# One decoder step on one core: the first norm worked tile by tile in the opening stage, the second at the end of the layer before it, and in the attention stage the sigmoids issued head by head and the value quarters spread over a turn

## The reference, cut to what matters

```
h = x
# layer 0: gated matrix-memory mixer
h = h + mlstm(rmsnorm(h, norm_mix[0]) @ w_in_a, state) @ w_out_a
h = h + square(relu(rmsnorm(h, norm_mlp[0]) @ w_up[0])) @ w_down[0]
k, v = rmsnorm(h, norm_kv) @ w_kv               # shared, 16 heads of 64
# layer 1: stick-breaking attention over cached pages and new keys
q = rmsnorm(h, norm_mix[1]) @ w_q_b
z = q @ k.T / 8 + bias
A[t, s] = sigmoid(z[t, s]) * prod_{s<j<t} (1 - sigmoid(z[t, j]))
h = h + (A @ v) @ w_out_b
h = h + square(relu(rmsnorm(h, norm_mlp[1]) @ w_up[1])) @ w_down[1]
y = rmsnorm(h, norm_final)
```

## Time and profile before

| what | before |
|---|---|
| median of 3 runs | 3087.38 us (3086.38 to 3090.63) |
| the profiled execution's own time | 3094.23 us |
| its span, first to last instruction | 3092.4 us |
| PE busy | 2893.2 us, 94% of the span |
| mean granted PE clock | 0.974 |

### The profile page before, as it was taken

The page is one execution under the profiler, slowest core; times in us unless marked ns, Lnnn a source line. Parts: engine busy times, 40 slices in busy tenths (PEclk is TensorE's granted clock), DMA queues, the critical chain, the costliest instruction groups (busy, mean ns, idle before and its releaser), DMA issues. The chain is left out here.

```text
span 3092.4 us, 49344 instructions
## 1 busy us (share of the span) xinstructions
PE 2893.2 (94%) x19749; PEld 2634.2 (85%) x19749; DVE 1378.7 (45%) x1993; ACT 818.4 (26%) x1647; POOL 756.2 (24%) x452
## 2 busy tenths in 40 slices
PE   5999997999999999978999899898799999999998
PEld 4989887999999999976766677666599999999997
DVE  4422334444433344444546554655545433344434
ACT  3120222211110011124555545555512110011112
POOL 4212111322323323332111211120122332332331
PEclk8999998999999999989999999999899999999999
DMA  5666444233233232223333433343411111111112
GB/s 160 177 149 193 83 29 92 73 92 96 81 95 95 81 95 87 89 97 96 107 109 98 121 97 114 100 119 91 147 48 42 48 42 47 47 41 47 47 41 77
DMA packets 362482, 277.68 MB, mean 90 GB/s; under 512 B 31394, under 2 KB 353954, under 8 KB 360290
## 3 DMA queue, kind: packets, MB, share of 16 engines
q1 hardware_dynamic: 341002, 258.18, 28.8%
q10 hardware_dynamic: 21336, 17.47, 2.9%
HBM read 251.58 MB, written 91.11 MB: 111 GB/s over the span
## 5 line engine op out<-in xcount | busy, mean ns | idle before, releaser
L162 POOL CAST w_hi<-w_raw 128x1024 fp32r<-128x1024 f32 x194 | 208.6, 1075 | 1661.1 <-PE bank L214 902.0
L212 PE MATMUL bank<-p_u_hi,w_hi 128*128 128x352 f32 x1536 | 496.5, 323 | 14.5 <-DVE p_u_lo L2001 14.5
L212 PE MATMUL bank<-x_hi,w_hi 128*128 128x352 f32 x1536 | 496.9, 323 | 2.9 <-DVE p_q L1758 2.9
L213 PE MATMUL bank<-p_u_lo,w_hi 128*128 128x352 f32 x1536 | 495.5, 323 | 0.0
L214 PE MATMUL bank<-p_u_hi,w_lo 128*128 128x352 f32 x1536 | 495.3, 322 | 0.0
L214 PE MATMUL bank<-x_hi,w_lo 128*128 128x352 f32 x1536 | 494.5, 322 | 0.0
L213 PE MATMUL bank<-x_lo,w_hi 128*128 128x352 f32 x1536 | 494.0, 322 | 0.0
L164 POOL TENSOR_TENSOR w_lo<-w_raw,w_hi 128x1024 fp32r<-128x1024 f32 x194 | 483.8, 2494 | 15.6
L2009 DVE TENSOR_TENSOR h<-bank,h 128x352 f32<-128x352 f32 x384 | 199.9, 524 | 492.5 <-PE bank L214 492.5
L1961 ACT ACTIVATE p_relu<-bank 128x352 f32<-128x352 f32 x192 | 89.1, 464 | 1039.5 <-PE bank L214 1033.2
L212 PEld LDWEIGHTS bank<-p_u_hi,w_hi 128*128 128x128 f32 x1536 | 288.5, 188 | 18.7 <-issue 18.7
(11 more groups left out here) (247 smaller groups left out, 4587.7 us busy)
## 6 DMA issues: line engine op xcount, KB each, us to landing
k_pages<-in_cache_k SPq DMA_DIRECT2D x64, 512.0 KB, 5.7
w_raw<-in_w_up SPq DMA_DIRECT2D x64, 512.0 KB, 4.0
v_pages<-in_cache_v SPq DMA_DIRECT2D x64, 512.0 KB, 4.8
w_raw<-in_w_down SPq DMA_DIRECT2D x64, 512.0 KB, 3.4
p_pages<-k_pages SPq DMA_DIRECT2D x256, 128.0 KB, 2.4
p_pages<-v_pages SPq DMA_DIRECT2D x256, 128.0 KB, 2.3
w_raw<-in_w_in_a SPq DMA_DIRECT2D x26, 512.0 KB, 4.5
h<-h_spill ACTq DMA_DIRECT2D x16, 528.0 KB, 8.6
```

Of the source, the lines that this page charges most:

```text
L162: pool.tensor_copy(m.whi[slot][:, :], m.wraw[slot][:, :]).then_inc(w.hi, 1)
L212: pe.matmul(bank[:, 0:TW], wh, xh, start=(k == 0), stop=False)
L213: pe.matmul(bank[:, 0:TW], wh, xl, start=False, stop=False)
```

## The change

Four parts.

**Start.** `constants` and `embed` become one stage, `start`. The rows of `x` are the first transfers, the first weight panel comes in after the third block of them, one gain goes out on ACT's queue, the rest at the end of SP's. ACT copies two of every three turned halves, DVE one. As soon as the tokens of a tile of 352 are there, ACT and DVE make its `x_hi` and `x_lo` and PE its share of the gate product (banks 5 to 7); squares are added per tile. Ln and Exp of the norm stand at the stage's end, and SP writes the copy of `h` that the next stage needs. `mixer_a` no longer has a norm or the unused second panel, and takes its first dense tile (TAU0) ahead of the gate rows.

**Handover.** In layer 0's MLP the last of the 8 turns is written out. In it ACT and DVE follow each finished block `k` with `x_hi`, `x_lo`, square and sum, SP stores the block, and PE ends the stage with `dense_first` for `mixer_b` in banks 5 to 7, the sum over partitions (banks 2 to 4) ahead of its last two blocks. `mixer_b` begins with tile 3.

**Sigmoids.** ACT's sigmoids for a chunk are issued one head at a time with a turn's copy in between, where both heads' stood together.

**Order in a slot.** In slots 1 and 5 the value quarters stand after turns 0, 1 and 3 and at the end, where they stood after turns 0 to 3. In slots 0 and 4 DVE takes `chain_of` of the first chunk ahead of `chain_sample`.

```diff
+    VALUES_AFTER = {0: [0], 1: [1], 3: [2]}
...
-                    if i < len(quarters):
-                        values(*quarters[i])
+                    for x in VALUES_AFTER.get(i, ()):
+                        if x < len(quarters):
+                            values(*quarters[x])
...
-                if tiles:
-                    gates(p, n, 0)
+                due = [(x, h2) for x in range(len(CHUNKS[n])) for h2 in range(2)] if tiles else []
+                if due:
+                    gates(p, n, *due.pop(0))
                 for i, y in enumerate(turns):
                     read_turn(y)
-                    if i == 1 and lower:
-                        gates(p, n, 1)
+                    if due and (due[0][0] == 0 or i):
+                        gates(p, n, *due.pop(0))
...
-                for pc, g in at(SUMS_AT, slot):
-                    chain_sample(pc, g)
                 done = []
...
                 if p < PAIRS:
                     chain_of(p, n, 0)
+                for pc, g in at(SUMS_AT, slot):
+                    chain_sample(pc, g)
...
+            if norm_after:
+                turn(CH - 1, 0)
+
+                def sums():
+                    pe.wait_ge(w.tile_free[2], USES_OUT + CH * USES_C)
+                    norm_pe(pe, m, after.s, 2)
+                dense_first(pe, m, after.w, 0, 0, 0, after.s.x, between=sums, at=KT - 2, bank0=5)
...
+                    if ending:
+                        dve.wait_ge(after.s.hi, k + 1)
+                        dve.tensor_tensor(m.xlo[:, k, :], m.h[:, k, :], f32(m.xhi[:, k, :]), ALU.subtract).then_inc(after.s.x, 1)
+                        norm_add(dve, m, after.s, k)
...
+            for g in range(2 * TO[1]):
+                turn(g)
+            gates(0)
+            for g in range(2 * TO[1], 2 * NB):
+                turn(g)
+            gates(1)
+            pe.wait_ge(made, 2)
+            wait_taken(pe, 2 * NB)
+            sums(0)
+            gates(2)
+            sums(1)
+            sums(2)
...
+            copies(0)
+            high(0)
+            copies(1)
+            high(1)
+            square(0)
+            copies(2)
+            high(2)
+            square(1)
+            square(2)
+            act.wait_ge(made, 2)
+            norm_act_rs(act, m, s, 2)
```

More of the change, by code:

```diff
@@ L111, in weight_turns @@
         per, per_tiles = len(panels), sum(x[1] for x in panels)
-        assert per % 2 == 0
+        assert per % 2 == 0 or (turns == 1 and panels is stages[-1][1])
         def turn(i, last, n0=n, t0=tiles, panels=panels, per=per, per_tiles=per_tiles):
@@ L236, in dense_first @@
     for k in range(KT):
-        if k == KT // 2 and between is not None:
+        if k == at and between is not None:
             between()
@@ L363, in _ @@
                 keep(v, ALU.is_equal, NEG, j, [[SG, 2], [-1, SB], [0, ST]], 0)
[L365 to L371, removed]
-                    sp.dma_start(tile[:, :], src.rearrange("(k p) -> p k", p=P)).then_inc(landed, 16)
-            sp.dma_start(m.ptab[:, :], m.d["page_table"].rearrange("b (o g) -> o (b g)", o=1)).then_inc(landed, 16)
-            sp.wait_ge(landed, 16 * len(gains) + 16)
@@ L378, in embed @@
[L378 to L396 removed]
+            split(1)
@@ new lines, in sums @@
+            def sums(t):
+                pe.wait_ge(s.acc, t + 1)
+                pe.matmul(m.bank[2 + t][:, 0:TW], m.ones[:, :], m.acc[:, t * TW:(t + 1) * TW], start=True, stop=True)\
+                    .then_inc(s.sum, 1)
+            for g in range(2 * TO[1]):
[7 more added lines that the diff above has]
+            sums(0)
@@ L1603, in turns @@
                     z(p, n, 1)
-                for y in quarters[len(turns_of(slot)):]:
+                placed = sum(len(x) for i, x in VALUES_AFTER.items() if i < len(turns_of(slot)))
+                for y in quarters[placed:]:
                     values(*y)
@@ L1832, in _, with out_and_mlp @@
                         sample_queries(pq)
-def out_and_mlp(nc, m, own, w_out, w_up, w_down, gain, gather, head, after):
+def out_and_mlp(nc, m, own, w_out, w_up, w_down, gain, gather, head, after, norm_after):
     with ExitStack() as c:
@@ L1963, in _ @@
                         act.activation(sqr[t][:, :], relu[t][:, :], ACT.Square).then_inc(sq_ready, 1)
+            with act.Fori(0, CH - norm_after) as i:
+                turn(i)
+            if norm_after:
+                turn(CH - 1)
+                for k in range(KT):
+                    for t in range(NT):
+                        act.wait_ge(w.tile_free[t], USES_OUT + (CH - 1) * USES_C + UT + k + 1)
+                    act.activation(m.xhi[:, k, :], m.h[:, k, :], ACT.Copy).then_inc(after.s.hi, 1)
+                    norm_square(act, m, after.s, m.h, k)
+                norm_act_rs(act, m, after.s, 2)
         @block.vector
@@ L1991, in _, with turn @@
             dve.wait_ge(s.rs, 1)
-            with dve.Fori(0, CH) as i:
+            def turn(i, ending):
                 for u in range(UT):
```

312 lines of the change are left out of this document (192 added, 120 removed).

## The result

The changed kernel is slower: 3114.43 us median of 4 runs (3110.65 to 3117.24), where the kernel before took 3088.77 beside it. The ratio is 1.0083 (1.0065 to 1.0100), 25.7 us. The profiled execution took 3111.77 us with a span of 3110.0 us, 17.6 us more than before. Stage lengths are compared between the two profiled executions.)

What follows compares the result with a forecast made beforehand. PE was taken as the bound, busy 2893.2 us, so only its idle or low-clock stretches could shrink. -17 - 24.5 + 27 = -14.5 us from the median 3087.4 gave 3073 us, range 3030 to 3091 (8 in 10).

Steps and rivals of the forecast that it cites:

- quarters: Slots 1 and 5 of `mixer_b`: new places save 14 of 17.1 us of value-page waits; order in front costs 2 back.
- heads: Slot 3 of `mixer_b`: sigmoids by head shorten the `follow` wait and low clock, saving 17 us; slot 2 nothing.
- the discount: `mixer_b`: 13 us taken off the +40 loss, as other engines run on while PE waits at `sat`.
- Term 1: The start: earlier `x` transfers and norm work end the pick product near 52 us, -17 us, bounds -11 and -24.
- Term 2: Handover from layer 0's MLP to `mixer_b`: PE works on without the idle stretch, -24.5 us, bounds -20 and -27.
- 3 us of cover: Start of `mixer_b`: panel 2 is ready near 1374 us, before PE asks for it at 1377, so no wait.
- Term 3: `mixer_b`: savings in waits against a late `sat`, a net loss of +27 us, bounds -17 and +45.
- The wait at `sat`: Slots 0 and 4 of `mixer_b`: PE waits 6.6 and 2.9 us, 48 + 23 us; low clock adds 16.
- `chain_of` first: Slot 1 of `mixer_b`: weights and sigmoids found ready, saving 10 of 14.7 and 8 of 11.1 us of waits.
- Rival (b): `mixer_b` loses from 41.5 us on, as the `sat` wait is paid in full; 3096 us at +50; chance 0.11.
- full price of +40: `mixer_b`: sum of all its savings and losses, +40 us, before 13 us were taken off.
- Rival (a): `mixer_b`: without turn-taking `sat` is hardly late, a wait of 1.6, 35 us less loss, 3037 us; chance 0.27.

Runs made afterwards that it cites:

- e1: The changed kernel with DVE taking the sample's scan and product ahead of the heads' again in slots 0 and 4: 3044.92 us.
- e4: The changed kernel with DVE's order, quarter places and sigmoids by head all undone, leaving the new start and handover: 3061.98 us.
- e8: e1 with the three bias transfers moved behind the weight panels and the first eight page loads of `mixer_b`: 3041.32 us.
- e5: The changed kernel with the sample's work ahead of the heads' in slot 0 only: 3079.43 us.
- e3: The changed kernel with both heads' sigmoids issued together again: 3110.29 us.
- e11: e1 with the value quarters back behind turns 0 to 3, so sigmoids by head remain: 3055.76 us.
- e12: e1 with both heads' sigmoids together again, so the quarters' new places remain: 3047.03 us.
- e13: The changed kernel with POOL holding back slot 0's panel split until DVE's sample product is done: 3097.54 us.
- e6: The changed kernel with the sample's work ahead of the heads' in slot 4 only: 3078.10 us.

## Why the prediction was wrong, point by point

**In short.** The forecast was a gain of 14.5 us, the result a loss of 25.7. Three steps failed. By the medians of e1 and e4: start and handover gave 24.5 us where I had 41.5; DVE's order cost 69.5 where I had 48 + 23 - 18 + 16 = 69 and took 13 off, 56; quarters and heads together gave 17.1 (e4 against e1) where I had 14 - 2 + 17 = 29. (-24.5 + 69.5 - 17.1 = 27.9, against 25.7 in the first measurement.) The direction was lost by the discount together with the other two; with 69 in place of 56 alone the sum would still have been a gain, of 1.5 us.

**Term 1, right.** -17 predicted, -15.9 measured, with errors that cancel: the stage ended at 46.1 where I had 42, the picks began 6.4 us behind it where I had 7 to 9 and ended near 55 where I had 52, 14.2 us sooner than before; another 1.7 us came behind them.

**Term 2, its price.** Tile 3 came 36.1 us sooner, within the 35 to 45 that I gave, so 20.2 us without the start, where the working had 22.0. (22.0 and the 2.9 of clock are 24.9, not 24.5.) What failed is the next step, "what is late next is panel 2", with 3 us of cover. It sends the load out at 1361.3 + 1.9 and has landing and three passes done near 1374, 10.8 us later; POOL's passes took 5.5 after the change, so 5.3 were left for landing. The trace of before had this panel's landing at 13.3 us, and the same slow queue ahead of it:

```profile
1356.17 7.01 SPq L1372 DMA_DIRECT2D w_raw<-in_w_q_b  x1
...
w_raw<-in_w_kv SPq DMA_DIRECT2D x1, 512.0 KB, 13.3
```

With that row the cover of 3 us becomes a lack of 5. Before, the small bias transfers and the first panels were hidden behind PE's 37 us of waiting and `dense_first`; with these gone, the queue is what PE waits for: 5.56 us, and low clock behind it (0.87 up to the first scores, where e8 has 1.00). e8 shows the cause, since with the bias behind the pages the wait is gone and the first scores come 33.4 us behind tile 3 instead of 40.6 (34.7 before). The handover was worth 20.2 - 6.0 = 14.2 us up to the first scores, not 24.5; with the bias late it would be 20.2 + 1.3 = 21.5.

**Term 3, the discount.** The wait at `sat` was predicted in full: 48 + 23 = 71 us, measured 71.8 in 16. It was mostly 5.5 to 6.0 us in slot 0 and 2.8 in slot 4 where I had 6.6 and 2.9; the first pair had 7.6, and the last 4.5 and 5.0 where I had 2 and 2.9. The other rows: the waits for value pages gave 5.2 us for my 12; the heads 2.3 at `follow` and 6.4 at the cached pages, 8.7 for my 17; `chain_of` first 10.9 + 5.7 = 16.6 for my 18. The sum of the waits is 71.8 - 5.2 - 8.7 - 16.6 = 41.3 us, against 39.7 more idle time; with 9.1 of lower clock (I had 16) it makes the 48.9.

The step that failed is "part of what the late `sat` costs is slack elsewhere ... I take 13 off": nothing came off. e1 tests it, since it differs from the changed kernel in the order alone. The waits behind copies, from which I took the 13, are 36.0 us in e1 (21.3 + 5.3 + 9.4) and 36.9 with the late `sat` (22.0 + 5.5 + 9.4). What a late `sat` does take over is the waits at `pack` and the scores (22.0 us, e1), which my sum already had as the 18; and e5 shows that slot 4's wait takes over nothing. Without the discount the price of the order, 69, is what e1 measured, 69.5 us.

**Term 3, the heads.** This is the term that was mis-sized. What it named came: slot 3 went from 14.7 to 12.6 us in six pairs, 13.9 in all, though not by this edit alone (by head against together it is 8.0 with the new quarters). (The term's pieces, 1.1 of wait and 1.5 of clock, would be 2.6 and not 2.1.) Slot 2 was put at nothing, and nearly so it was: what the copies of cached pages gained there came back at `follow`. What has no term is that the same edit lengthens the waits for value pages and for the sigmoids by 9 us together. By the runs the heads lie between a loss of 4 us (e3) and a gain of 6 (e11 against e4), not 17. The quarters were priced rightly, 14 us of page waits (19.4 to 5.3, e4 and e12) and 10.6 to 15 by the runs for my 12; that only 5.2 of page waits went from before to after is the heads' doing.

**The rivals.** Rival (b) happened: from tile 3 to the output projection, as the prediction measures it, `mixer_b` is 897.9 us instead of 843.0, 54.9 more, of which 6.0 are the page wait and its clock. I gave it 0.11 although my own full price of +40 stood 1.5 us from its threshold. The argument against it, that a late PE lets the other engines catch up, had no row behind it. Rival (a)'s number for a world without turn-taking, a wait of 1.6 us in slot 0, is close to what e13 measured (1.40); but its 35 us do not follow, since the hold-up moves to the next scans. e1 shows what the whole change without this order is worth: 3044.9 us, and e8 3041.3, the fastest of the kernels run here.

## What to carry to other kernels

An instruction moved to the back of a queue costs its consumer the length of what now stands ahead, less the slack that it had, and that length is read at the place where it runs: beside a GpSimd pass VectorE's scans and products took two to three times as long. Slack that a new wait may use up is counted once, from the waits just behind it, and a wait that PE had not had before is priced with the lower clock behind it (71.6 us of stage time for 50.3 us of idle time). A copy that is made earlier is priced at the place where PE waits next, too. Where a barrier's cover is removed, the first transfers behind it are what can be late next, and their landing times are read from the trace that has them (13.3 us here), not taken as short because nothing waited for them.

## What the runs showed of the hardware

- Three transfers of the bias, 12 KB in all, ahead of two panels of 512 KB made the first panel land in 13.1 us instead of 5.5, and the second panel's issue took 6.10 us instead of 0.57 (the changed kernel and e8). Before had it too: 13.3 and 7.01 us.
- Waits of 1.65 and 1.85 us at the same place were followed by a granted clock of 1.00 and of 0.53 (e1 and e8). Of 10.2 us that e8 lost behind its first scores, 6.2 were busy time at the lower clock.
- The price of a wait followed the idle time that was left after what it took over: 24.3 us of waits in slot 4 and 46.0 in slot 0 cost the same, 34.5 and 33.2 us, with 27.3 and 24.4 us more idle time and 10.6 and 12.9 us more busy time (e5, e6, e1).
- GpSimd's three passes lengthened two VectorE products and one scan by 4.6 us; held back, they lengthened the next two scans instead, from 2.33 to 4.80 us (the changed kernel and e13).
